# One tuned decoder kernel: the common product routine with both its column patterns reversed

## What is computed

```python
def swiglu_ffn(h, w_in, w_out):
    gate, up = jnp.split(h @ w_in, 2, axis=-1)
    return (jax.nn.silu(gate) * up) @ w_out
...
    for i in range(DEPTH):
        x = x + 0.5 * swiglu_ffn(rmsnorm(x, ffn1_norm[i]), ffn1_w_in[i], ffn1_w_out[i])
        h = rmsnorm(x, mix_norm[i])
        mk, mv = jnp.split(mem_n @ mem_w_kv[i], 2, axis=-1)
...
            z = h @ hgrn_w_in[j]
...
            z = h @ gmlp_w_in[j]
...
        o_mem = memory_attention(zx, mk, mv)
        x = x + jnp.concatenate([o_mix, o_mem], axis=-1) @ w_out
        x = x + 0.5 * swiglu_ffn(rmsnorm(x, ffn2_norm[i]), ffn2_w_in[i], ffn2_w_out[i])
    return rmsnorm(x, final_norm)
```

## Time and profile before

| | |
|---|---|
| median of 3 runs | 2354.65 us (2350.22 to 2355.73) |
| the profiled execution | 2353.23 us, span 2351.5 us |
| TensorE busy | 2328.8 us (99%), 11040 matmuls |
| VectorE busy | 1233.5 us (52%) |
| ScalarE busy | 764.4 us (33%) |
| GpSimd busy | 264.5 us (11%) |
| mean granted TensorE clock | 0.997 of full |
| HBM traffic over the span | 99 GB/s |

### The profile page before, as it was taken

The page is one execution under the profiler, slowest core; times in us unless marked ns, Lnnn a source line. Parts: engine busy times, 40 slices in busy tenths (PEclk is TensorE's granted clock), DMA queues, the critical chain, the costliest instruction groups (busy, mean ns, idle before and its releaser), DMA issues.

```text
span 2351.5 us, 29800 instructions
## 1 busy us (share of the span) xinstructions
PE 2328.8 (99%) x11040; PEld 1947.6 (83%) x11040; DVE 1233.5 (52%) x1467; ACT 764.4 (33%) x1045; POOL 264.5 (11%) x236
## 2 busy tenths in 40 slices
PE   9999999999999999999999999999999999999998
PEld 9988888878888888888878888888888888888887
DVE  6654443467888654444445444336437644444422
ACT  4432222244445322222222222224433222222322
POOL 3400001111333420000110000120001212000000
PEclk9999999999999999999999999999999999999999
DMA  7733333332222333333333333333232233333322
GB/s 235 215 98 95 93 97 99 95 104 69 72 71 80 99 97 92 97 98 98 98 90 90 98 98 98 97 92 107 72 99 85 86 98 99 99 98 97 92 95 92
DMA packets 400693, 234.35 MB, mean 100 GB/s; under 512 B 7692, under 2 KB 386672, under 8 KB 400624
## 3 DMA queue, kind: packets, MB, share of 16 engines
q1 hardware_dynamic: 397328, 223.37, 32.1%
q0 software_dynamic: 3280, 10.02, 1.2%
q10 hardware_dynamic: 16, 0.00, 0.0%
HBM read 227.07 MB, written 6.29 MB: 99 GB/s over the span
## 4 chain that ended last, share of the span: by engine, by line
PE 92%; DVE 4%; ACT 2%; issue 1%; DMA 1%; POOL 0%; DVEq 0%; ACTq 0%; SPq 0%; POOLq 0%
PE acc L1093 26%; PE acc L1094 26%; PE acc L1095 26%; PE acc L847 1%; PE acc L846 1%; PE acc L848 1%; ACT w_hi L1528 1%; DVE w_lo L1255 1%; PE acc L262 1%; PE acc L264 1%; PE acc L263 1%; PE mix L264 1%; PE mix L262 1%; PE mix L263 1%; DMA raw<-in_mem_w_kv_dram 1%
## 5 line engine op out<-in xcount | busy, mean ns | idle before, releaser
L1255 DVE TENSOR_TENSOR w_lo<-raw,w_hi 128x1024 fp32r<-128x1024 f32 (+1 forms) x422 | 544.9, 1294 | 636.2 <-ACT w_hi L1528 623.1
L1093 PE MATMUL acc<-h_hi,w_hi 128*128 128x512 f32 x1920 | 756.0, 394 | 7.6 <-DVE h_lo L1318 5.3
L1094 PE MATMUL acc<-h_lo,w_hi 128*128 128x512 f32 x1920 | 748.5, 390 | 0.0
L1095 PE MATMUL acc<-h_hi,w_lo 128*128 128x512 f32 x1920 | 748.4, 390 | 0.0
L1528 ACT ACTIVATE w_hi<-raw 128x1024 fp32r<-128x1024 f32 (+1 forms) x422 | 436.4, 1038 | 341.7 <-DMA raw<-in_ffn_w_out_dram 219.6
L1093 PEld LDWEIGHTS acc<-h_hi,w_hi 128*128 128x128 f32 x1920 | 361.5, 188 | 84.4 <-DVE h_lo L1318 6.6
L1094 PEld LDWEIGHTS acc<-h_lo,w_hi 128*128 128x128 f32 x1920 | 361.5, 188 | 75.4 <-issue 2.0
L1095 PEld LDWEIGHTS acc<-h_hi,w_lo 128*128 128x128 f32 x1920 | 361.2, 188 | 75.4
L1093 PE MATMUL acc<-act_hi,w_hi 128*128 128x512 f32 (+1 forms) x976 | 367.6, 377 | 1.9 <-DVE w_lo L1255 1.2
L1095 PE MATMUL acc<-act_hi,w_lo 128*128 128x512 f32 (+1 forms) x976 | 365.7, 375 | 0.0
L1094 PE MATMUL acc<-act_lo,w_hi 128*128 128x512 f32 (+1 forms) x976 | 365.7, 375 | 0.0
(11 more groups left out here) (243 smaller groups left out, 1895.0 us busy)
## 6 DMA issues: line engine op xcount, KB each, us to landing
raw<-in_ffn_w_in_dram SPq DMA_DIRECT2D x176, 512.0 KB, 3.7
raw<-in_ffn_w_out_dram SPq DMA_DIRECT2D x70, 512.0 KB, 3.4
raw<-in_hgrn_w_in_dram SPq DMA_DIRECT2D x40, 512.0 KB, 3.7
raw<-in_gmlp_w_in_dram SPq DMA_DIRECT2D x40, 512.0 KB, 3.6
raw<-in_mem_w_kv_dram SPq DMA_DIRECT2D x32, 512.0 KB, 4.4
raw<-in_gmlp_w_out_dram SPq DMA_DIRECT2D x24, 512.0 KB, 3.4
raw<-in_ffn_w_out_dram SPq DMA_DIRECT2D x24, 384.0 KB, 3.0
raw<-in_hgrn_w_out_dram SPq DMA_DIRECT2D x16, 512.0 KB, 3.4
```

The source lines that it names most:

```text
L1093: pe.matmul(bank, top[:, i, :], hi, start=(start and i == 0), stop=False)
L1094: pe.matmul(bank, top[:, i, :], lo, start=False, stop=False)
L1095: m = pe.matmul(bank, rest[:, i, :], hi, start=False, stop=(stop and i == last))
L1255: dve.tensor_tensor(lane_of(w_lo, q, j)[:, 0:nkb], lane_of(raw, q, j)[:, 0:nkb], f32(lane_of(w_hi, q, j)[:, 0:nkb]), ALU.subtract).then_in ...
```

## The change

In `unit`, the moving operand is read with a step of -1 from its last column to its first, and the result is written into the bank with a step of -1 from its last column to its first. Stationary operands, waits, increments, and the start and stop flags are as before. Since both patterns are reversed, each column of the product ends where it did. The two programs have the same instructions in the same order on every engine: 5659 rows in TensorE's list with its loops rolled up, and no difference in any list but in the steps of these three lines.

```diff
@@ -1090,9 +1090,9 @@
                 for i, (hi, lo) in enumerate(operands):
                     if each:
                         each(i)
-                    pe.matmul(bank, top[:, i, :], hi, start=(start and i == 0), stop=False)
-                    pe.matmul(bank, top[:, i, :], lo, start=False, stop=False)
-                    m = pe.matmul(bank, rest[:, i, :], hi, start=False, stop=(stop and i == last))
+                    pe.matmul(bank[:, ::-1], top[:, i, :], hi[:, ::-1], start=(start and i == 0), stop=False)
+                    pe.matmul(bank[:, ::-1], top[:, i, :], lo[:, ::-1], start=False, stop=False)
+                    m = pe.matmul(bank[:, ::-1], rest[:, i, :], hi[:, ::-1], start=False, stop=(stop and i == last))
                 m.then_inc(unit_done, 1)
```

## The result

The changed kernel takes 2401.98 us (median of 4 runs, 2400.83 to 2403.15) against 2354.08 us for the kernel before (4 runs, 2350.22 to 2355.73). The ratio is 1.0206, 95% interval 1.0188 to 1.0224: about 48 us slower. The forecast was 2354 us, no change.

A forecast was written before the change was run, and what follows sets the result against it. The prediction took TensorE to bound the kernel, its routine matmuls taking 1927.7 us of the 2351.5 us span. Every part of the change counted 0, so 2353.23 us + 0 = 2353 us, given as 2354; range 2347 to 4080 us.

The forecast's parts named there:

- What bounds the kernel: TensorE, busy 99% of the span, decides the time; any change per matmul is multiplied by 8688.
- The write to PSUM and the readers, 0 each: Writing result columns last to first costs 0; VectorE's reads wait for the whole matmul, so also 0.
- The fetch, 0: In the routine's 8688 matmuls, fetching the moving operand from column 511 down to 0 costs 0 ns.
- The 8.5 ns that don't depend on the columns: Of 226.7 ns between starts of 512-column matmuls, 218.2 are the column stream and 8.5 ns are independent of columns.
- The small cost: Longer set-up at the far end of each matmul's pattern, 6.6 ns each, 57 us: 2361 to 2411 us; chance 0.10.
- The half rate: Columns pair only when ascending, in fetch or PSUM write, so all 8688 matmuls halve their rate: 4045 to 4070 us; chance 0.25.
- The rival that the change doesn't do what it says: A build cancels both reversals, so time stays within 0.3%; shares chance 0.56 with no cost at all.
- faster: The other order avoids the 8.5 ns beyond the columns in each matmul, 74 us in all: 2279 us; chance 0.05.

The follow-up runs named there:

- write_only: The kernel before with only the PSUM bank written downwards, the moving operand read upwards: 2354.20 us, ratio 1.0001.
- fetch_only: The kernel before with only the moving operand read downwards, the bank written upwards: 2401.62 us, ratio 1.0201.
- elems_down: The kernel before with the moving operand's 16-byte groups read first to last, the 4 values inside each downwards, bank written upwards: 2353.65 us, ratio 1.0005.
- lines_down: The kernel before with the moving operand's 16-byte groups read last to first, the 4 values inside each upwards, bank written upwards: 2400.41 us, ratio 1.0197.
- groups256_down: The kernel before with the second half of the moving operand's columns read before the first, both upwards: 2354.74 us, ratio 1.0004.
- shift32_down: The kernel before with fetch and write both descending and the weights 128 bytes further up: 2411.94 us, ratio 1.0241.

## Why the prediction was wrong

**What bounds the kernel**: right. TensorE decides the time, and the extra busy time of TensorE is the extra span, 49.9 us each. Multiplying a change in the distance of starts by the number of matmuls was the way to cost it: 8304 x 6.67 ns = 55 us, against the 48 measured. What it left out are two waits and the clock after them, which gave some 4 us back.

**The write to PSUM and the readers, 0 each**: right, shown by write_only (2354.20 us).

**The fetch, 0**: this is the step that failed. It costs 6.7 ns for each matmul of 512 columns, and fetch_only alone shows the whole loss, 47 us. The reason given for 0 was that any two columns that follow each other are still neighbours in memory. elems_down breaks that neighbourhood and costs nothing, and lines_down keeps it inside 16 bytes and costs everything. What decides is the order in which stretches of 16 to 128 bytes follow each other; at 512 bytes it no longer matters, and between 128 and 512 nothing was tried.

**The 8.5 ns that don't depend on the columns**: wrong, and it could have been seen in the trace before. I took the 256-column distance from one stretch, 117.6 ns. A stretch of the same lines at 15 us, where the matmuls and weight loads look the same, has (17.32 - 15.28) / 18 = 113.3 ns, exactly half of 226.7. This is the timeline of the kernel before:

```profile
15.28 0.28 PE L1095 MATMUL acc<-act_hi,w_lo 128*128 128x256 f32 x1
...
17.32 0.28 PE L1095 MATMUL acc<-act_hi,w_lo 128*128 128x256 f32 x1
```

So at its best the fetch takes 1/16 more than 213.3 ns for 512 columns and 106.7 ns for 256 (both at 2.4 GHz). These two distances are in proportion to the columns and leave no fixed part, though the weights of the 256-column matmuls lie 64 bytes further up, so the two aren't quite alike. One kind of matmul with two distances in one trace was the hint that the distance has several states, and that a change in the order of the fetch might leave the best one. In the changed kernel the 256-column matmuls are partly at 120 ns, (30.00 - 28.20) / 15:

```profile
28.20 0.28 PE L1094 MATMUL acc<-act_lo,w_hi 128*128 128x256 f32 x1
...
30.00 0.28 PE L1094 MATMUL acc<-act_lo,w_hi 128*128 128x256 f32 x1
```

**The rivals.** The small cost had a chance of 0.10 and the range 2361 to 2411 us; the time fell into it. Its size, 6.6 ns, came from the earlier trace rows and is what was measured, but by luck: those rows are from the uneven start after another line's matmuls (224 to 236 ns in the trace), which is back at 226.7 ns within ten matmuls, while the reversed fetch stays at 233.3 ns throughout. Its reason, a longer set-up at the far end, is refuted: groups256_down also starts far from the first column and costs nothing. The half rate (0.25) did not happen in any form: no variant has a mean distance above 237 ns. The rival that the change doesn't do what it says fell, since fetch_only costs as much as the full change, and "faster" fell too. The range, 2347 to 4080 us, held the time but said little; the forecast inside it was no change, and the kernel is clearly slower.

**What stays open.** What in the fetch stalls isn't settled. The runs allow a conflict in SBUF that depends on the order of addresses within some hundred bytes, on the place of the weights, and on a timing that the weight load influences; no run shows such a conflict itself. No test left the weight load out, moved the activations in place of the weights, or stopped the other engines that use SBUF beside TensorE.

## What to carry to other kernels

The matmuls here are float32r ones (the kernel's F32R buffers; the rows print them as f32). For such a matmul, read the moving operand upwards, or at least in stretches of 512 bytes; here the order inside 16 bytes and the direction of the write to PSUM were free. In a kernel that TensorE bounds, compare the distance of two starts with columns divided by the clock, and if it is more than 1/16 above, try other places for the weights: here 64 bytes alone cost 47 us, and 256 bytes nothing. With a descending fetch no place helped. And when one shape shows two distances in one trace, take neither for a constant.

## What the hardware showed that I had not expected

- The distance of the same matmul, 128x512 at the full clock, holds one of several values over long stretches: 226.7 or 233.3 ns, or a mean of 229 to 231 or 236.7 to 236.9 ns, by the order of the fetch and the place and length of the weight load. In shift32_down it goes from 236.9 to 233.3 ns within one trace, with all of these unchanged.
- Moving the weights by 64 bytes cost the ascending kernel 47 us (2401.58 against 2354.15 us); moving them by 256 bytes cost nothing.
- Shortening the weight loads made the ascending kernel slower: 2369 us with 64 columns, 2374 us with 4, against 2353 to 2354 us with 128.
- A write to PSUM with a step of -1 is as fast as one with +1: 2354.20 against 2354.15 us.
